# A two-block network on one core: stabiliser rows fetched by DMA, transposes ahead of a stage's last tile, output products among attention units

## The reference, cut to what matters

```
def mlstm_chunkwise(q, k, v, i_pre, logf): ...     # layer 0, four heads
    D = b[..., :, None] - b[..., None, :] + ic[..., None, :]      # causal
    m_s = jnp.maximum(m_inter, D.max(axis=-1))
    wts = jnp.exp(D - m_s[..., None]) * (q @ k.T)
    h = num / jnp.maximum(jnp.abs(den), jnp.exp(-m_s))[..., None]
def dilated_layer(h, k, v, ...):                    # layer 1, four heads
    # three windows with dilations 1, 4, 16; softmax over all their keys
    y = o * jax.nn.silu(z);  return y @ w_out
def ple_add(h, p_l, norm_g, w_gate, w_proj):        # after each layer
    gate = jax.nn.sigmoid(rms_norm(h, norm_g) @ w_gate)
    return h + (p_l @ w_proj) * gate
```

## Time and profile before

| | |
|---|---|
| median of 3 runs | 1586.98 us (1585.86 to 1587.59) |
| profiled execution | 1587.24 us |
| its span, first to last instruction | 1585.5 us |
| PE busy | 1539.6 us, 97% of the span |
| PE weight loads | 1257.4 us, 79% |
| VectorE, GpSimd, ScalarE busy | 718.5, 695.0, 592.2 us |
| mean granted TensorE clock | 0.996 |
| PE busy in 1440 to 1480, 1480 to 1520 | 34.29 and 35.79 of 40 us |
| PE busy in 1160 to 1200 | 37.72 of 40 us, clock 0.92 |

### The profile page before, as it was taken

How to read it: one execution, slowest core, us unless ns; L and a number is a source line. 1 busy time by engine, 2 the same in 40 slices (tenths; PEclk the granted TensorE clock), 3 DMA queues, 4 the chain that set the end, 5 groups by cost and what they waited for, 6 DMA issues and landing times.

```text
span 1585.5 us, 19734 instructions
## 1 busy us (share of the span) xinstructions
PE 1539.6 (97%) x7593; PEld 1257.4 (79%) x7593; DVE 718.5 (45%) x1189; ACT 592.2 (37%) x902; POOL 695.0 (44%) x309
## 2 busy tenths in 40 slices
PE   7999999999999999999999999999999999998898
PEld 6877866877888888888888888888867788887677
DVE  4158854482334236556563006710163446354553
ACT  5353254572333324212212116322243455365342
POOL 5423455334555536344344344443422345446432
PEclk9999999999999999999999999999999999999999
DMA  7323211102333323333332225544211322322021
GB/s 235 112 67 130 83 54 48 41 21 77 100 99 99 109 90 94 106 96 89 106 94 92 107 58 80 115 98 106 83 64 32 101 80 80 112 88 80 1 80 53
DMA packets 144390, 137.21 MB, mean 87 GB/s; under 512 B 7696, under 2 KB 118160, under 8 KB 144316
## 3 DMA queue, kind: packets, MB, share of 16 engines
q1 hardware_dynamic: 140676, 130.79, 28.7%
q10 hardware_dynamic: 3640, 5.40, 1.0%
HBM read 134.05 MB, written 2.12 MB: 86 GB/s over the span
## 4 chain that ended last, share of the span: by engine, by line
PE 86%; DVE 4%; ACT 3%; POOL 3%; issue 2%; DMA 1%; SPq 0%; DVEq 0%; ACTq 0%; POOLq 0%
PE banks L712 83%; POOL w_lo L563 1%; PE banks L736 1%; PE banks L882 1%; ACT w_hi L1408 1%; DMA raw<-in_w_mem_kv 1%; POOL w_lo L546 1%; PE banks L1298 0%; DVE resid L2178 0%; ACT k L1821 0%; ACT junk L1673 0%; DVE prob L2427 0%; POOL stick_a L600 0%; ACT junk L1666 0%; DVE head_ms L2375 0%
## 5 line engine op out<-in xcount | busy, mean ns | idle before, releaser
L546 POOL TENSOR_TENSOR w_lo<-raw,w_hi 128x2048 fp32r<-128x2048 f32 x105 | 485.8, 4627 | 616.9 <-ACT w_hi L1408 616.9
L712 PE MATMUL banks<-h_hi,w_hi 128*128 128x512 f32 (+1 forms) x904 | 348.1, 385 | 3.3 <-DVE h_lo L1957 0.9
L712 PE MATMUL banks<-h_hi,w_lo 128*128 128x512 f32 (+1 forms) x904 | 340.4, 377 | 0.0
L712 PE MATMUL banks<-h_lo,w_hi 128*128 128x512 f32 (+1 forms) x904 | 340.1, 376 | 0.0
L1408 ACT ACTIVATE w_hi<-raw 128x2048 fp32r<-128x2048 f32 x126 | 238.8, 1895 | 211.6 <-PE banks L712 201.7
L712 PEld LDWEIGHTS banks<-h_hi,w_hi 128*128 128x128 f32 x904 | 169.9, 188 | 43.8 <-issue 9.7
L712 PE MATMUL banks<-w_hi,h_hi 128*128 128x512 f32 (+1 forms) x544 | 199.3, 366 | 0.0
L712 PE MATMUL banks<-w_hi,h_lo 128*128 128x512 f32 (+1 forms) x544 | 198.1, 364 | 0.0
L712 PE MATMUL banks<-w_lo,h_hi 128*128 128x512 f32 (+1 forms) x544 | 198.1, 364 | 0.0
L712 PEld LDWEIGHTS banks<-h_hi,w_lo 128*128 128x128 f32 x904 | 169.7, 188 | 32.1
L712 PEld LDWEIGHTS banks<-h_lo,w_hi 128*128 128x128 f32 x904 | 169.9, 188 | 29.2
(11 more groups left out here) (311 smaller groups left out, 2361.3 us busy)
## 6 DMA issues: line engine op xcount, KB each, us to landing
raw<-in_w_in SPq DMA_DIRECT2D x56, 512.0 KB, 4.0
raw<-in_w_ffn_in SPq DMA_DIRECT2D x44, 512.0 KB, 5.0
raw<-in_w_in_a SPq DMA_DIRECT2D x32, 512.0 KB, 5.7
raw<-in_w_ffn_out SPq DMA_DIRECT2D x22, 512.0 KB, 3.9
raw<-in_w_ple_gate SPq DMA_DIRECT2D x16, 512.0 KB, 4.6
raw<-in_w_in_b SPq DMA_DIRECT2D x16, 512.0 KB, 4.4
raw<-in_w_mem_kv SPq DMA_DIRECT2D x8, 512.0 KB, 5.6
raw<-in_w_out SPq DMA_DIRECT2D x8, 512.0 KB, 3.6
```

What stands on the lines that cost most here:

```text
L546: pool.tensor_tensor(slot_of(w_lo, slot), slot_of(raw, slot), slot_of(w_hi, slot).bitcast(F32), ALU.subtract).then_inc(lo_made, 1)
L712: return pe.matmul(out, lhsT, rhs, start=start, stop=stop, **kw)
```

## The change

Five edits, all in the second block.

1. **Stabiliser rows.** The four `pick` products are gone, and with them the constant and its load. ScalarE's queue writes `m_row` to a DRAM scratch (8 KB) before stage `o2`, and after `o2` reads it back in four DMAs, each of which puts one row on all 128 partitions (`m_all`, 256 KB each). ScalarE's exponentials read `m_all` in place of PSUM bank 3. The wait for the DMAs (`row_in`, 64) stands ahead of the first of them.
2. **Denominators.** VectorE waits for all four tiles of a head, takes the three small operations once for 128x4 elements, and then the four 128x256 operations. `y_lo` of column tiles 2 and 3 now comes ahead of the last head's denominators, and `y_hi` of both ahead of its squares.
3. **Gate seams.** The transposes of column tiles 0 and 1 stand ahead of the plain stage's last token tile, in banks 0 and 1, which its first tile used. ScalarE and VectorE copy them out ahead of the last tile; ScalarE's split of the second gate slab comes after column tiles 2 and 3.
4. **Attention units.** The split of the second `wout3` slab moves: ScalarE's copy from ahead of the units to the end of step 6, GpSimd's subtraction from ahead of the units into quarters in steps 8, 9, 12 and 13. VectorE scales ahead of the least value in the steps with s % 4 of 0 or 3.
5. **Output products.** Those of head 0 stand in steps 17 (three tiles) and 18 (one), those of head 1 in step 19 (two tiles) and after it (two).

```
-                mm(banks[:, 3, :], pick[0:4, h * P:(h + 1) * P], m_row[:], True, True).then_inc(m_s, 1)
+        act.wait_ge(m_rows, 2)
+        act.dma_start(row_scratch.ap(), m_row[:]).then_inc(row_out, 16)
         for c in range(2):
             split_group("o2", c)
             sigmoid_group("o2", c, 1 - c, o2)
+        act.wait_ge(row_out, 16)
+        for h in range(4):
+            act.dma_start(m_all[h][:], row_scratch.ap()[h].partition_broadcast(P)).then_inc(row_in, 16)
...
+                dve.wait_ge(m_out, 4 * h + 4)
+                link(dve.scalar_tensor_tensor(out=den_h, in0=sums, scalar=-1.0, in1=em_h, op0=ALU.mult, op1=ALU.max))
+                link(dve.tensor_tensor(den_h, sums, den_h, ALU.max))
+                link(dve.reciprocal(inv_h, den_h))
                 for t in range(NT):
-                    dve.wait_ge(m_out, 4 * h + t + 1)
-                    link(dve.tensor_scalar(den[:, i4], banks[:, 4 + t, 256:257], -1.0, em_col[:, i4], ALU.mult, ALU.max))
-                    link(dve.tensor_tensor(den[:, i4], banks[:, 4 + t, 256:257], den[:, i4], ALU.max))
-                    link(dve.reciprocal(den_inv[:, i4], den[:, i4]))
...
+                    if n == 1 and (q, t) == (0, NT - 1):
+                        ahead_of_last()
...
+            gemm_whole(plain_stage, p_hi, p_lo, ahead_of_last=lambda: rows_ahead(0, 2))
+            rows_ahead(2, 2)
...
-        split_lo(BASE["z3"] + 2, BASE["wout3"] + 2)
+        split_lo(BASE["z3"] + 2, BASE["wout3"] + 1)
         for step in range(16):
+            if step in (8, 9, 12, 13):
+                lo_quarter(BASE["wout3"] + 1, (8, 9, 12, 13).index(step))
...
+            if step == 17:
+                pe.wait_ge(at_neg, U_D + 15)
+                head_products(0, range(3))
+            if step == 18:
+                pe.wait_ge(at_neg, U_D + 16)
+                head_products(0, (3,))
+            if step == 19:
+                head_products(1, range(2))
...
         for step in range(16 + LAG_OUT):
+            probs_first = step % 4 in (0, 3)
+            if probs_first and 2 <= step <= 17:
+                unit_probs(step)
             if step < 16:
+                unit_least(step)
+            if not probs_first and 2 <= step <= 17:
+                unit_probs(step)
```

More of the change, by code:

```diff
@@ L148, in constants @@
         dil[:, 256 + 512 * i:768 + 512 * i] = np.where((dist >= 0) & (dist % r == 0), 0.0, NEG)
[L149 to L153, removed]
+    return {"c_sq": sq.reshape(P, -1), "c_onehot": onehot, "c_rope": rope, "c_dil": dil}
 def head_and_tile(n):
@@ L336, in _program @@
     i_row, f_row, nf_row, a_row, m_row, em_row = rows4
+    m_all = [arena(f"m_all{h}", 75 + 2 * h, S) for h in range(3)] + [place("m_all3", 106.5, S)]
     y2_hi, y2_lo = arena("y2_hi", 0, KD * S, F32R), arena("y2_lo", 65, KD * S, F32R)
@@ L1092, in _, with gemm_whole @@
                 gate_slab(i, s)
-        def gemm_whole(stage, x_hi, x_lo, ready=None):
+        def gemm_whole(stage, x_hi, x_lo, ready=None, ahead_of_last=None):
             n = COUNT[stage]
@@ L1252, in gated_addition, with rows_ahead @@
         def gated_addition(g_name, gate_stage, plain_stage, p_hi, p_lo, between=None):
[L1253 to L1258, removed]
+            def rows_ahead(first, count):
+                for k in range(first, first + count):
+                    bank = transposed_bank(g_name, k)
+                    emptied, table = (ev_v, EV_V) if bank % 2 else (ev_a, EV_A)
+                    pe.wait_ge(emptied, table[plain_stage] + bank // 2 + 1)
+                    transposes(g_name, rows_of(xs), 1, first=k)
+            gemm_whole(plain_stage, p_hi, p_lo, ahead_of_last=lambda: rows_ahead(0, 2))
+            rows_ahead(2, 2)
             wait_emptied(EV_A[gate_stage], EV_V[gate_stage])
@@ L1345, in d_logits, with head_products @@
             return ins
-        for step in range(16 + LAG_OUT):
+        g = BASE["wout3"]
+        out_hi, out_lo = (slot_of(w, g % 2).rearrange("p (k c) -> p k c", k=4) for w in (w_hi, w_lo))
+        def head_products(k, tiles):
+            pe.wait_ge(lo_made, g + 1)
+            pe.wait_ge(at_lo, 8 + k + 1)
+            for t in tiles:
+                at_ = slice(k * S + t * P, k * S + (t + 1) * P)
+                ins = mm3(banks[:, t, :], y3_hi[:, at_], y3_lo[:, at_], out_hi[:, k, :], out_lo[:, k, :], k == 0, k == 3)
+                if k == 3 and t < NT - 1:
+                    ins.then_inc(tile_done, 1)
+            return ins
+        for step in range(16 + LAG_OUT):
+            if step == 17:
[6 more added lines that the diff above has]
+                head_products(1, range(2))
             if step in (1, 3):
@@ L1759, in _ @@
                     split_hi(0, "wout2", 0)
+            if step == 5:
+                transposed_hi("y2", 4, V_HEAD, y2_hi, first=2)
             if step >= 2:
@@ L1767, in _ @@
                                          accum_out=head_ss[:, 4 * h + t:4 * h + t + 1])
-                    if (step, t) == (5, 2):
-                        transposed_hi("y2", 4, V_HEAD, y2_hi, first=2)
                 ins.then_inc(m_ss, 1)
```

114 lines of the change are left out of this document (55 added, 59 removed).

## The result

| | before | after |
|---|---|---|
| time, median of 6 runs (us) | 1587.51 (1585.86 to 1591.88) | 1576.58 (1573.27 to 1580.25) |
| profiled execution (us) | 1587.24 | 1576.76 |
| its span (us) | 1585.5 | 1575.0 |
| PE busy in it (us) | 1539.6 | 1535.0 |
| lost in it at half clock (us) | 5.04 | 3.25 |

The change makes the kernel faster: ratio 0.9923, 95% interval 0.9911 to 0.9934. The forecast was 1576.5 us with a range of 1572.5 to 1581.0. Without it the two spans are 1580.5 and 1571.75 us; I call such a number the clock-free span, and a stretch of several windows with the clock down a spell.

A forecast was written before the change was run, and what follows sets the result against it. PE was taken as the bound, busy 1539.6 of 1585.5 us, so only its waits, work and clock give time. Gains 5.7 + 6.45 + 0.15 - 1.75 = 10.55 us gave 1576.5 us, range 1572.5 to 1581.0.

The forecast's parts named there:

- mLSTM: mLSTM: 1.8 us earlier wout2 start plus 2.1 us y_lo wait removed; 5.7 us gained including a half-clock spell.
- units: Attention units: waits removed at start, middle and end, 2.8 + 0.3 + 1.6 us; 6.45 gained including a spell.
- seams: Gate seams: waits exchanged for others of the same length, 0.1 us gained at each seam, half-clock spell apart.
- clock: PE's half-clock spells, 1.74 us each: gone behind y_lo and at the units' end, one new for two seams.
- Start: Start of the attention units: the 2.25 us wait and most of the 0.87 go, 2.8 us gained.
- End: End of the attention units: output products fill waits, a bank 7 wait of some 1.6 us appears; 1.6 us gained.
- Middle: Middle attention units: scaling ahead of the least value, 0.3 us gained; bounds 1.3 gained to 2 lost.
- The quarters: Rival, attention units: GpSimd's four quarter splits each delay a scaling by up to 1.3 us; 1581.6 us, chance 0.07.
- every long wait: Rival: clock falls at both seams and again at the units' end, behind the bank 7 wait; 1580.0 us, chance 0.20.
- none: Rival: no half-clock spell at the seams or after the mLSTM's first head; 1573.0 us, chance 0.17.
- Rows late: Rival, mLSTM: the four row DMAs land late, stopping ScalarE and PE; 1598 us at 45 us, chance 0.03.
- Given back: Rival: earlier PE meets later engines in wout2 or the next projections; about 1586.5 us, chance 0.03.

The follow-up runs named there:

- the second profile: The changed kernel, unaltered, executed again beside a run with the gate seams as before; measured 1578.54 us, ratio 0.9947.
- the late split alone: The kernel before with only the split of the second output slab moved into steps 6 to 13 of the attention units; 1585.48 us, ratio 0.9988.
- with the least value first: The changed kernel with VectorE taking the next unit's least value ahead of the scaling in all steps, as before; 1576.14 us, ratio 0.9929.
- seam as before: The changed kernel with all gate-seam transposes after the last token tile again; 1573.25 us, ratio 0.9915, and 1575.10 us, ratio 0.9925, when repeated.
- the kernel with GpSimd's waits: The changed kernel with GpSimd's first gate-slab subtraction waiting for all four VectorE scalings xs; 1570.14 us, ratio 0.9895.

## Why the prediction was right

Clock-free gains by the stretches of the table above, against the prediction's terms with their spells taken out:

| | forecast (us) | measured (us) | from |
|---|---|---|---|
| ahead of the mLSTM | 0 | -0.3 | 1151.67 less 1151.96; executions differ (1151.72 in the second profile) |
| mLSTM | 3.95 | 4.9 | 48.67 less 43.79 |
| units | 4.7 | 4.4 | 74.37 less 69.97 |
| seams | 0.15 | -0.3 | 243.87 less 244.04, and 61.88 less 61.99 |
| clock | 1.75 | 1.8 | 5.04 less 3.25 |
| sum | 10.55 | 10.5 | 1587.24 less 1576.76 |

The steps of the mechanism held in each of the terms. That the sum came out within 0.1 us is luck: the mLSTM gave 0.9 more than forecast, and the other rows 1.0 less. So is the closeness of the median, 1576.58 against 1576.5: five more executions of the same kernel had one of 1578.54.

*mLSTM.* The steps held: the logits wait at the second head, the start of `wout2` (1184.65; forecast 1186.7 with a spell of 1.74 in it, so 1184.96), the end of the wait for `y_lo`. The term was too small where I let new waits take 0.65 of the 2.45 us back. From the start of the mLSTM to `wout2` it took 35.2 us before and 32.7 after, so 2.5 gained instead of 1.8; the one new wait there is 0.32 us, where one of 0.16 had been.

*Units.* Start 2.8 forecast, 3.12 - 0.28 = 2.84 measured, of which the late split alone gives 1.9. End 1.6 forecast, 3.27 - 1.66 = 1.61 measured. Middle 0.3 forecast, nothing measured: 0.26 + 0.68 + 1.04 + 0.68 = 2.66 us of waits now, 2.65 before. The quarters did meet scalings, and held them, but not for their whole length. VectorE and GpSimd, changed kernel:

```profile
1451.18 0.42 DVE L2449 TENSOR_SCALAR prob<-prob,inverse 128x384 f32<-128x384 f32 x1 [0.93 <-POOL prob L703]
1461.49 1.23 DVE L2449 TENSOR_SCALAR prob<-prob,inverse 128x384 f32<-128x384 f32 x1
1464.18 0.65 DVE L2449 TENSOR_SCALAR prob<-prob,inverse 128x512 f32<-128x512 f32 x1
```
```profile
1461.16 1.35 POOL L701 TENSOR_TENSOR prob<-prob 128x512 f32<-128x512 f32 x1 [1.69 <-ACT prob L1903]
```

The same 128x512 scaling with the least value first, and the quarter beside it:

```profile
1464.52 1.12 DVE L2449 TENSOR_SCALAR prob<-prob,inverse 128x512 f32<-128x512 f32 x1
```
```profile
1464.08 1.27 POOL L561 TENSOR_TENSOR w_lo<-raw,w_hi 128x512 fp32r<-128x512 f32 x1
```

A 128x512 scaling takes 0.49 us where it meets nothing (unit 15). The quarter that runs from 1463.27 to 1464.55 makes it 0.65: the scaling began late in the quarter. With the least value first it began earlier in it and took 1.12. PE waited for neither, since its transposes of those units have no wait. Two of the four quarters met one. Far more often GpSimd's sums hold the scalings: 0.42 us became 1.23 beside the sum from 1461.16 to 1462.51, and this scaling ends the 0.68 us wait of unit 6. In each such row the scaling ends 0.1 to 0.3 us after GpSimd does. The rule on mutual exclusion (the Trainium skill, SBUF — State Buffer, Who interferes with whom) agrees with these rows, and with the seams: 5.1 us beside a subtraction, 0.75 us when it waits. What the units would gain if the sums kept clear of the scalings was not tried.

*Seams.* What a seam takes is the same within 0.2 us, as predicted, though the wait of 2.1 us in one piece came as four pieces, 1.57 us in all, because each transpose of the first column tile waits for its own scaling. But I took what I saw there, the 5.1 us scaling, as given, and did not price its removal; it was the limit of the stage.

*Clock.* Here two misses cancelled. The forecast kept a spell behind the first head's wait and put one at the seams; the first profile had none and two. The second profile of the changed kernel has one behind the first head and one at a seam (1158 and 1518), just as forecast. So in the first profile the number was right and the places were not. This is the term that a profile of one execution cannot give. Over all profiles, how many of each wait were followed by half clock:

| wait of PE | followed by half clock |
|---|---|
| 2.50 us after the first head's logits (no `pick`) | 7 of 9 |
| with `pick`: 0.87 us ahead of the first head, 0.84 or 0.60 behind it | 4 of 4, in two already behind the first |
| 2.12 us for `y_lo` | 4 of 4 |
| 1.05 and 1.97 us at the end of the units | 4 of 4 |
| 1.05 us there without the 1.97 | 0 of 2 |
| 2.25 and 0.87 us at their start | 3 of 4 |
| seam as changed, four pieces of 1.6 us in all | 4 of 6 |
| seam as before, 0.70 and 1.38 us | 0 of 14 |
| the same place, 2.27 us | 1 of 2 |
| 1.66 us at unit 12's values | 0 of 8 |

The rivals "every long wait" and "none" were thus not two worlds but single runs of one kernel: spans of 1578.5 and 1571.5 us among the first six. Of the eleven executions of the changed kernel five lie within the forecast's 1574.5 to 1578.5 us, four above and two below; the range holds all of them.

*Rows late.* The four DMAs were issued from 1108.6 to 1109.9 and landed 3.8 us later, 40 us ahead of their use at 1154.1. I had placed the issue at 1130.6, because I took the earlier trace rows for the last sigmoid of `o2`. Its output is `z`, so it belongs to the stage after. The last one of `o2` in the kernel before is this:

```profile
1108.26 0.60 ACT L1478 ACTIVATE o<-banks 128x512 f32<-128x512 f32 x1 [2.12 <-PE banks L712]
```

The slip was harmless: the cover was larger than counted.

*Given back* did not happen.

## What to carry over

Price the clock apart from the waits, and as a chance, from several executions: a wait of 2 us on a full PE cost either 2 or 3.7 us here. When a change at a seam only exchanges waits, look for the late producer behind all of them; here one GpSimd operation beside VectorE's scalings made the seam, and two waits on GpSimd turned an edit worth nothing, or less than that by its spells, into 2.4 us a seam. Compare parts by the stretch of the trace in which they act, not by whole spans: one profile whose first load came 1.8 us late made a part worth 2.6 us look like 0.8. And do not take a spell's full price off a wait behind it, since a slower PE can swallow that wait.

## What the runs showed of the hardware

- The same waits in the same kernel were followed by half clock in some executions and not in others. More idle time alone does not decide it: at the old seams 2.1 idle of 6 us never did it, at the new ones 1.6 us in four pieces mostly did, and two waits under 0.9 us around the first head did it in all four profiles that have them. What does was not settled.
- Runs of one kernel differ by steps of 1.7 us, the price of one spell: the kernel with GpSimd's waits has spans of 1568.3, 1568.4, 1568.4 and 1570.1, 1570.3 us.
- A scaling of 128x1024 float32 on VectorE took 5.1 us beside a GpSimd subtraction of 4.9 us and 0.75 us without; the subtraction itself went from 4.94 to 4.61 us. Short operations do the same: a 128x384 scaling took 1.23 us beside a sum of 1.35 us and 0.42 us without.
- The first load of an execution was late once: PE's first instruction waited 10.5 us for it, where it waited 8.6 to 9.1 us in the other thirteen profiles.
- A matmul of 128 columns by 512 in plain float32 took 0.85 us, against 0.23 us from start to start in the split products.
